# Moving the key copies, the key turnings and three exponentials inside a hand-written schedule of a hybrid decode step

## The chip, the cores and the metric

One core of one Trainium2 chip runs the whole step. The time is device microseconds of one launch. The kernel before takes 2246.21 us, the median of 3 runs (2242.72 to 2254.63).

## The reference: what is computed

One layer of a decoder with two head groups, for one new sequence of 512 tokens and for 8 decoding sequences with 4096 past tokens each. The part that matters here is, for each decoding sequence `b`, the attention over its paged cache (`cmp_attention`, `select_blocks` and `selected_attention` of the reference):

```
kc, vc = compress(cached keys), compress(cached values)   # windows of 32 rows, step 16
p_cmp  = softmax(q kc / 8);  o_cmp = p_cmp vc              # 255 compressed positions
imp    = group sums of p_cmp over blocks of 64 tokens
sel    = top_k(imp, 16)                                    # 3 blocks are forced
o_slc  = softmax(q k[sel] / 8) v[sel]                      # 16 chosen blocks, 961 positions
o_win  = softmax(q k_win / 8) v_win                        # the newest 512 rows
o      = g0 o_cmp + g1 o_slc + g2 o_win
```

The compression is the heavy part: `silu(rows . w1 + pe . w1) . w2` over all 4096 cached rows of each sequence. All numbers are float32. After the 8 sequences comes the output projection with a residual sum and a layer norm.

## The kernel before, in words

Three phases follow each other: the recurrent heads and the prompt (about the first 950 us), a middle phase to about 1150 us, and `decode_output_phase`, to which the change belongs.

**The places.** The decode part is one stream on TensorE of `NSTEP` = 128 steps, 16 for each sequence (8 for keys, then 8 for values). A step has three matmuls of 128x512 (`product(s, 0)` to `product(s, 2)`, L1592). Each of these 384 matmuls is a place; a sequence has 48 places. Behind the matmul of a place TensorE may do a unit of turning (`turn`, L1569: four transposes of cached rows into one of two PSUM banks `tb`), which ScalarE copies to SBUF in two instructions (L1835), after which VectorE takes differences (L1941, L1944). Four units make a group `Q`, and a group feeds two steps. Units stand in four of six places, so that they have to go through two banks: TensorE may not write a bank before the copy of the unit or piece before it is done.

**The pieces.** The attention of each sequence is cut into pieces, and a table gives each the place where all engines do their part of it. `AT` counts from the sequence's own first place, so 48 to 95 lie beside the compression of the next sequence and from 96 on beside that of the one after it; `LAST` is the same table for sequence 7. The function `program` walks over the places, and each of TensorE, ScalarE and VectorE runs it with its own functions: first its part of the matmul, then its part of the turning, then of the piece. Since an engine works strictly in order, a piece whose input is late holds all that stands behind it on that engine.

The pieces that the change touches:

- `fetch0` to `fetch3`: of the 16 chosen blocks a quarter at a time. ScalarE copies the keys of the gathered rows to `Kc` (L1894, L1895, L1897) and VectorE the values to `Vg` (L2082 to L2090). Both wait for the gather of that quarter. GpSimd issues the gathers (`chosen`, L1536), 5 indirect DMAs for the first quarter and 8 for each other, into two buffers in turn: quarter 2 may start when quarter 0 is copied, quarter 3 when quarter 1 is.
- `keys0` to `keys3`: TensorE turns `Kc` (L1698) into a bank, and VectorE copies the bank to `KgT` (`empty_keys`, L1807). There is one `Kc`, so `fetch1` waits for the turning of `keys0`, and so on.
- `scores`, `SCORES`, `WSCORES`: TensorE multiplies keys with queries (L1649), VectorE takes the maximum and its negative (L2006, L2097, L2103 and the lines behind), ScalarE the exponential with its sum (L1869, L1874, L1879).

Around them stand `bend` (L1850), the sigmoid of the compression on ScalarE at the places 23, 24, 47 and 48 of a sequence, whose output `sg` lies in the same memory as `Kc`; `finish` (L1964) on VectorE, which reads `sg`; `join_sum` (L1958); `keep_sum` (L1842). ScalarE has to load a table (ACT_TABLE_LOAD) when it goes from sigmoid to exponential or back.

**The other queues.** GpSimd also gathers the cached rows of the next sequence (`rows`, L1514, 32 indirect DMAs a sequence into `Xr` and `xT`), a quarter of a buffer at a time as its turning is done, and it issues them in between the gathers of `chosen` in one fixed order. SyncE loads the newest rows of the next sequence when the window piece `WVALUES` of a sequence is done (`window`, L1443 to L1449: 1 MB in, then 1 MB out).

```
if key[..] in TURNS: n = used.index(min(used)); put(pieces[t], n)     # bank of a piece
act.wait_ge(*landed(b, q)); ...; need(act, hs_r, bends[0])            # fetch on ScalarE
if keyed[0]: act.wait_ge(tr[bank], k + 1)                             # bend: Kc must be turned
```

Of the kernel before, what the change touches and what calls it, by code (L numbers as in the profile page):

```python
# [620 lines left out]
def need(eng, sem, n):  # L621

    if n > 0:
        eng.wait_ge(sem, n)
# [606 lines left out]
def decode_output_phase(nc, io, keep):  # L1231
# [14 lines left out]
    NJ, NSTEP = CD // 2, NB * CD  # L1246
# [5 lines left out]
    with ExitStack() as ctx:  # L1252
# [30 lines left out]
        acc, om = [sb(f"acc{n}", [R, KVH * DH]) for n in range(2)], sb("om", [P, KVH * DH])  # L1283
# [53 lines left out]
        AT = {  # L1337
            ("second", 0): 27, ("second", 1): 29, "queries": 25, "scores": 31, "weights": 34, "turned": 36,
            "sums": 37, "first": 38, "values": 39, "slots": 40, "bases": 41, "rows": 45,
            ("second", 2): 51, ("second", 3): 53, "fetch0": 55, "mix": 56, "acc": 57, "keys0": 59,  # L1340
            "fetch1": 62, "keys1": 64, "fetch2": 70, "keys2": 71, "fetch3": 80, "keys3": 81,
            "SCORES": 94, "SCALE": 96, "TURNED": 98, "VALUES": 100, "NEWEST0": 106, "NEWEST1": 108,
            "WSCORES": 109, "WSCALE": 113, "WTURNED": 115, "WVALUES": 116, "SUM": 117, "DONE": 122,
        }
# [7 lines left out]
        pieces = {}  # L1352
        for b in range(NB):
            for key, t in (AT | (LAST if b == NB - 1 else {})).items():
                t += 3 * CD * b
                t = t if t < 3 * NSTEP else 3 * NSTEP + 2 * (t - 3 * NSTEP)
# [14 lines left out]
        def landed(b, q):  # L1371

            return g_in[q % 2], 16 * (TAKEN[q % 2] * b + sum(GATHERS[q % 2:q + 1:2]))
# [10 lines left out]
        FETCH = "fetch0", "fetch1", "fetch2", "fetch3"  # L1384
# [4 lines left out]
        def unit(t):  # L1389

            s, n = divmod(t, 3)
            if s % 2 == 1 and n == 2:
                Q, u = (s + 3) // 2, 0
            elif s % 2 == 0:
                Q, u = s // 2 + 1, n + 1
            else:
                return None
            return (Q, u) if Q < NSTEP // 2 else None
# [4 lines left out]
        for t in range(3 * NSTEP + KT * TILES):  # L1403
# [4 lines left out]
            if t in pieces and pieces[t][0] in TURNS:  # L1408
                n = used.index(min(used))
                put(pieces[t], n)  # L1410
                used[n] = 2 * t + 3

        def program(eng, do):

            for s in range(NSTEP):
                for n in range(3):
                    do["product"](s, n)
                    then = unit(3 * s + n)
                    if then:
                        do["turn"](*then)  # L1420
                    name, which = pieces.get(3 * s + n, (None, None))
                    if name in do:
                        do[name](which)
            for u in range(KT * TILES):
                i, k = divmod(u, KT)
                do["output"](i, k)
                name, which = pieces.get(3 * NSTEP + u, (None, None))
                if name in do:
                    do[name](which)
                if k == KT - 1:  # L1430
                    do["end"](i)
# [390 lines left out]
        def _(act):  # L1822
# [59 lines left out]
            def fetch(q):  # L1882


                def do(b):
                    act.wait_ge(*landed(b, q))
                    if 4 * b + q:
                        bank, k = place[QUARTERS[q - 1], b if q else b - 1]
                        act.wait_ge(tr[bank], k + 1)
                    need(act, hs_r, bends[0])  # L1890
                    keyed[0] = QUARTERS[q], b
                    KVq = buffer(b, q)
                    if q == 0:
                        A(Kc[:, 0], forced(KVq, 0), ACT.Copy)  # L1894
                        A(Kc[:, 1], KVq[:, 1, :, 0:DH], ACT.Copy).then_inc(k_c, 1)  # L1895
                    else:
                        A(Kc[:], KVq[:, :, :, 0:DH], ACT.Copy).then_inc(k_c, 1)  # L1897

                return do
# [14 lines left out]
            for u in range(4):  # L1914
# [2 lines left out]
            program(act, {  # L1917
                "product": product, "turn": turn, "output": output, "end": lambda i: None,
                "scores": scores, "SCORES": chosen_scores, "WSCORES": newest_scores,
                **{FETCH[q]: fetch(q) for q in range(4)}})  # L1920
            gather(0)
            root(0, 0, P)
            root(1, 1, P)
# [414 lines left out]
```

## Time and profile before

| | us |
|---|---|
| median of 3 runs | 2246.21 |
| lowest, highest run | 2242.72, 2254.63 |
| the profiled execution | 2249.45 |
| its span, first to last instruction | 2247.6 |
| TensorE busy in the span | 2016.1 |
| VectorE busy | 915.7 |
| ScalarE busy | 707.9 |
| GpSimd busy | 629.6 |

The profiled execution took 1.85 us more than its span, and 3.2 us more than the median run. The rows further down are of this one execution. Times in them count from the start of its span. The decode part's 384 matmuls run from 1166.7 to 1979 us. A group of rows names the engine, the line, the operation, what is written and read, and how many; in brackets is the idle time of the engine before it and what ended it. "issue" means that nothing the profile shows was waited for, and "remote" that the semaphore's last writer could not be matched.

### The profile page before, as it was taken

The page shows a single profiled execution, that of the slowest core. Times are in us where ns is not written, and L with a number is a line of the kernel's source. Part 1 is how long each engine was busy: PE and PEld are TensorE (multiplying, and loading weights), DVE is VectorE, ACT ScalarE, POOL GpSimd, SP SyncE. Part 2 cuts the span into 40 slices and gives each one's busy share as a digit, 9 for nine tenths or more (in the row PEclk, how much of TensorE's full clock was granted, in tenths as well). Part 3 has the DMA queues.
Part 4 walks back from the last instruction along what each step waited for, and adds up shares of the span by engine and source line. Part 5 has one row for each costly group of instructions (what it writes and reads, how often), then busy time and mean ns, then how long its engine had stood idle before and what let it go on. Part 6 is the DMA issues. An engine that isn't in the chain of part 4 may idle for free. (4 is left out here: it accounts for less than half of the span.)

```text
span 2247.6 us, 24649 instructions
## 1 busy us (share of the span) xinstructions
PE 2016.1 (90%) x9303; PEld 1372.5 (61%) x9303; DVE 915.7 (41%) x1821; ACT 707.9 (31%) x1297; POOL 629.6 (28%) x649
## 2 busy tenths in 40 slices
PE   8999999999999999999968778677687878899997
PEld 7888888888888877777634334333343434434442
DVE  0445355454510144444434344445353545432126
ACT  0233112332200032332335444445354544510013
POOL 0000000000020034343545465555565555240000
PEclk9999999999999999999979889898888998999999
DMA  5232222222232211111155253545454453564114
GB/s 202 67 101 77 85 85 77 94 75 85 77 111 76 93 61 57 38 57 38 54 177 146 76 159 90 179 121 165 134 144 142 139 155 119 164 234 155 75 75 151
DMA packets 71076, 247.86 MB, mean 110 GB/s; under 512 B 11220, under 2 KB 28832, under 8 KB 56768
## 3 DMA queue, kind: packets, MB, share of 16 engines
q1 hardware_dynamic: 38344, 139.10, 17.8%
q0 software_dynamic: 31360, 103.32, 15.7%
q10 hardware_dynamic: 1280, 4.23, 0.5%
q8 instruction: 57, 0.93, 0.2%
q14 instruction: 35, 0.29, 0.0%
HBM read 224.64 MB, written 21.96 MB: 110 GB/s over the span
## 5 line engine op out<-in xcount | busy, mean ns | idle before, releaser
L292 PE MATMUL pj<-xT,strips 128*128 128x260 f32 x2368 | 532.6, 384 | 6.4 <-DMA xT<-d_xT 6.4
L292 PEld LDWEIGHTS pj<-xT,strips 128*128 128x128 f32 x2368 | 445.9, 191 | 72.3 <-issue 6.3
L1835 ACT ACTIVATE big<-dtb 64x512 f32<-64x512 f32 x512 | 302.8, 591 | 314.6 <-PE dtb L1569 172.2
L792 PE MATMUL pj<-xT,strips 128*128 128x260 f32 x1216 | 292.0, 388 | 0.0
L1592 PE MATMUL dpH<-big,w 128*128 128x512 f32 x512 | 287.3, 658 | 0.4 <-DVE hs L1958 0.4
L792 PEld LDWEIGHTS pj<-xT,strips 128*128 128x128 f32 x1216 | 222.4, 190 | 59.8 <-issue 30.1
L1018 POOL MEMSET kbd<- 128x128 f32 x1 | 0.2, 205 | 635.4 <-POOLq L126 635.4
L1569 PEld LDWEIGHTS dtb<-const,xT 128*128 128x128 f32 x512 | 65.3, 150 | 181.5 <-issue 87.5
L1941 DVE TENSOR_TENSOR big<-big 128x512 f32<-128x512 f32 x128 | 88.3, 689 | 212.5 <-ACT big L1835 174.2
L1569 PE MATMUL dtb<-const,xT 128*128 128x128 f32 x512 | 84.7, 292 | 99.9 <-DVE KgT L1807 79.2
L1044 POOL TENSOR_SCALAR old<-old,rd 128x128 f32<-128x128 f32 (+3 forms) x116 | 122.2, 1068 | 166.6 <-DVE rd L1153 166.6
L1536 POOL DMA_INDIRECT KV<-d_cache,gi x104 | 105.7, 1016 | 166.9 <-DVE gi L2072 89.9
L1514 POOL DMA_INDIRECT Xr<-d_cache,row x128 | 134.0, 1047 | 41.7 <-issue 38.7
L1569 PEld LDWEIGHTS dtb<-const,Xr 128*128 128x128 f32 x512 | 69.3, 155 | 122.4 <-issue 90.5
L1592 PE MATMUL dpH<-big 128*128 128x512 f32 x256 | 140.4, 631 | 0.0
L1514 POOL DMA_INDIRECT xT<-d_cache,row x112 | 109.3, 976 | 92.9 <-PE dtb L1569 64.3
L1536 POOL DMA_INDIRECT oT<-d_cache,gi x112 | 108.6, 969 | 85.1 <-DVE Vg L2085 53.1
L1592 PEld LDWEIGHTS dpH<-big,w 128*128 128x128 f32 x512 | 90.2, 206 | 62.7 <-issue 51.5
L1569 PE MATMUL dtb<-const,Xr 128*128 128x128 f32 x512 | 87.3, 299 | 36.4 <-ACT big L1835 20.9
L1611 PE MATMUL dpH<-xT,oT 128*128 128x512 f32 x256 | 113.6, 596 | 0.0
L1611 PE MATMUL dpH<-Xr,oT 128*128 128x512 f32 x256 | 113.0, 596 | 0.0
L988 ACT ACTIVATE PT<-mpT 128x512 f32<-128x512 f32 (+2 forms) x48 | 25.3, 526 | 206.3 <-PE mpT L880 196.5
(311 smaller groups left out, 2402.1 us busy)
## 6 DMA issues: line engine op xcount, KB each, us to landing
strips<-d_w_in SPq DMA_DIRECT2D x60, 1024.0 KB, 5.3
xT<-d_w_out SPq DMA_DIRECT2D x16, 1024.0 KB, 7.5
d_win_sample<-Wt SPq DMA_DIRECT2D x8, 1024.0 KB
Xr<-d_w_out SPq DMA_DIRECT2D x8, 1024.0 KB, 10.1
Wt<-d_win SPq DMA_DIRECT2D x8, 896.0 KB
xT<-d_xT SPq DMA_DIRECT2D x8, 520.0 KB, 8.9
Sold<-d_state SPq DMA_DIRECT2D x8, 512.0 KB, 5.5
vB<-v_rows ACTq DMA_DIRECT2D x8, 512.0 KB, 7.0
```

What stands on the lines that cost most here:

```text
L292: mm = nc.tensor.matmul(pj[b][:, a, 0:TH], w[b][:, k, :], xT[:, k, a * TH:(a + 1) * TH], start=(k == 0), stop=(k == KT - 1))
L792: mm = nc.tensor.matmul(bank(s)[:, n, 0:TH], w[s % 2][:, k, :], xT[:, k, n * TH:(n + 1) * TH], start=(k == 0), stop=(k == KT - 1))
L988: nc.scalar.activation(blocks(brs, 0, qt), pT[:, 0:len(brs) * (qt + 1) * P].rearrange("p (r c n) -> p r c n", r=len(brs), n=P), ACT.Copy). ...
L1018: nc.gpsimd.memset(kbd[:], 0.0).then_inc(zr, 1)
L1044: ins = nc.gpsimd.tensor_scalar(p, p, rd[U % 4][:, k:k + 1], None, ALU.mult)
L1514: pool.indirect_dma_start(out=X[par][:, r, :], out_offset=None, in_=pairs, in_offset=bass.IndirectOffsetOnAxis(ap=row[:, 2 * b + par, r:r ...
L1536: pool.indirect_dma_start(out=to, out_offset=None, in_=heads, in_offset=bass.IndirectOffsetOnAxis(ap=gi[b % 2][0:n, a:a + 1], axis=0),).th ...
L1569: mm = nc.tensor.transpose(tb[bank][:, i * P:(i + 1) * P], X[par][:, r, (2 * kind + hp) * P:(2 * kind + hp + 1) * P], ident)
L1592: mm = nc.tensor.matmul(pH[n][:], left, right, start=(j == 0), stop=(j == NJ - 1))
L1611: mm = nc.tensor.matmul(pH[i % 2][:], oT[:, k, t * P:(t + 1) * P], wo[c % 2][:, k, :], start=(k == 0), stop=(k == KT - 1))
L1835: ins = A(dst[:, :, :, hd], tb[bank][hd * DH:(hd + 1) * DH].rearrange("p (j h n) -> p j h n", j=2, h=2), ACT.Copy)
L1941: V.tensor_tensor(D1[:, s], D2[:, s], Or[:, s], ALU.subtract).then_inc(diff_r, 1)
```

## The change

Nothing is computed otherwise, and no instruction of data is added or removed. Three things move:

1. In `AT` (sequences 0 to 6) the copies `fetch0` to `fetch3` go from the places 55, 62, 70, 80 to 54, 59, 66, 72, and the turnings `keys0` to `keys3` from 59, 64, 71, 81 to 55, 62, 70, 76. `LAST` stays.
2. `program` takes a table `later`. For ScalarE alone the exponentials of `scores`, `SCORES` and `WSCORES` are done one place after the place where the other engines do their part (for sequence 7 as well).
3. A place can now hold two pieces of one engine; they are done in the order of the table.

```diff
         AT = {
             ("second", 0): 27, ("second", 1): 29, "queries": 25, "scores": 31, "weights": 34, "turned": 36,
             "sums": 37, "first": 38, "values": 39, "slots": 40, "bases": 41, "rows": 45,
-            ("second", 2): 51, ("second", 3): 53, "fetch0": 55, "mix": 56, "acc": 57, "keys0": 59,
-            "fetch1": 62, "keys1": 64, "fetch2": 70, "keys2": 71, "fetch3": 80, "keys3": 81,
+            ("second", 2): 51, ("second", 3): 53, "fetch0": 54, "keys0": 55, "mix": 56, "acc": 57,
+            "fetch1": 59, "keys1": 62, "fetch2": 66, "keys2": 70, "fetch3": 72, "keys3": 76,
             "SCORES": 94, "SCALE": 96, "TURNED": 98, "VALUES": 100, "NEWEST0": 106, "NEWEST1": 108,
             "WSCORES": 109, "WSCALE": 113, "WTURNED": 115, "WVALUES": 116, "SUM": 117, "DONE": 122,
         }
...
-        def program(eng, do):
-
+        def program(eng, do, later={}):
+
+            due = {}
+            for t, (name, which) in pieces.items():
+                if name in do:
+                    due.setdefault(t + later.get(name, 0), []).append((name, which))
             for s in range(NSTEP):
                 for n in range(3):
                     do["product"](s, n)
                     then = unit(3 * s + n)
                     if then:
                         do["turn"](*then)
-                    name, which = pieces.get(3 * s + n, (None, None))
-                    if name in do:
+                    for name, which in due.get(3 * s + n, ()):
                         do[name](which)
...
-                **{FETCH[q]: fetch(q) for q in range(4)}})
+                **{FETCH[q]: fetch(q) for q in range(4)}}, {"scores": 1, "SCORES": 1, "WSCORES": 1})
```

## Rows read from the trace of the kernel before

**Rows 1.** The page's first part: busy time, share of the span, instructions of each engine

```profile
PE 2016.1 (90%) x9303; PEld 1372.5 (61%) x9303; DVE 915.7 (41%) x1821; ACT 707.9 (31%) x1297; POOL 629.6 (28%) x649
```

**Rows 2.** Stretches of 48 places: length, busy us of each engine, clock, DMA share, GB/s

```profile
1567.00:1673.50 106.50, 81.50 (x344) 42.26 (x343) 48.11 (x106) 51.53 (x85) 59.87 (x61) 0.89 0.48 141
...
1882.00:1979.00 97.00, 80.09 (x323) 39.76 (x322) 45.93 (x102) 46.80 (x77) 32.14 (x33) 0.91 0.50 174
```

**Rows 3.** Waits of TensorE from 950 to 2100 us: total us, times, longest

```profile
PE dtb L1569 <- DVE KgT L1807: 79.2, 20, 12.6
...
PE dtb L1698 <- ACT Kc L1897: 22.6, 14, 2.6
```

**Rows 4.** Timeline round a `keys3`, places 31 to 35: start, us, engine, line

```profile
1538.80 1.28 ACT L1869 ACT_TABLE_LOAD   x1
...
1541.89 0.63 ACT L1897 ACTIVATE Kc<-oT 128x512 f32<-128x512 f32 x1
...
1542.58 0.99 PE L1698 MATMUL dtb<-const,Kc 128*128 128x128 f32 x4 [2.15 <-ACT Kc L1897]
...
1545.63 0.66 PE L1569 MATMUL dtb<-const,xT 128*128 128x128 f32 x4
```

**Rows 5.** Timeline round a `keys1`, places 16 and 17

```profile
1604.76 0.66 PE L1698 MATMUL dtb<-const,Kc 128*128 128x128 f32 x4 [1.08 <-ACT Kc L1897]
...
1607.82 0.66 PE L1569 MATMUL dtb<-const,xT 128*128 128x128 f32 x4 [1.54 <-DVE KgT L1807]
```

**Rows 6.** Timeline round a `keys2`, places 22 to 24: SyncE, TensorE, GpSimd, VectorE, ScalarE

```profile
1506.44 0.32 SPq L1443 DMA_DIRECT2D Wt<-d_win  x1
...
1508.75 0.60 PE L1698 MATMUL dtb<-const,Kc 128*128 128x128 f32 x4
...
1509.51 0.96 POOL L1514 DMA_INDIRECT xT<-d_cache,row  x1 [0.30 <-issue]
...
1522.06 0.69 DVE L1807 COPY KgT<-dtb 128x512 f32<-128x512 f32 x1 [9.79 <-remote]
1522.13 1.28 ACT L1850 ACT_TABLE_LOAD   x1 [14.22 <-remote]
...
1522.81 1.11 PE L1569 MATMUL dtb<-const,xT 128*128 128x128 f32 x4 [12.60 <-DVE KgT L1807]
```

**Rows 7.** TensorE's timeline at the same place of three other sequences

```profile
1416.52 1.12 PE L1569 MATMUL dtb<-const,xT 128*128 128x128 f32 x4 [12.02 <-DVE KgT L1807]
...
1838.26 1.11 PE L1569 MATMUL dtb<-const,xT 128*128 128x128 f32 x4 [10.43 <-issue]
...
1935.35 0.66 PE L1569 MATMUL dtb<-const,xT 128*128 128x128 f32 x4 [1.98 <-DVE KgT L1807]
```

**Rows 8.** Two stretches from a window load on, as in the view of rows 2

```profile
1506.40:1522.80 16.40, 3.81 (x15) 1.78 (x13) 5.77 (x10) 1.79 (x3) 9.79 (x11) 0.75 0.91 273
...
1929.60:1945.00 15.40, 11.49 (x45) 5.20 (x43) 10.89 (x24) 8.36 (x13) 2.15 (x3) 1.00 0.83 257
```

**Rows 9.** Timeline from `SCORES` on, place 46 to place 1 of the next sequence

```profile
1567.26 1.06 ACT L1874 ACTIVATE pg<-dpS,col 40x961 f32<-40x961 f32 x1 [4.51 <-DVE col L2098]
...
1568.43 1.28 ACT L1850 ACT_TABLE_LOAD   x1
1569.73 0.72 ACT L1850 ACTIVATE Kc<-hs,hb 128x512 f32<-128x512 f32 x1
...
1571.44 0.71 ACT L1850 ACTIVATE Kc<-hs,hb 128x512 f32<-128x512 f32 x1
...
1571.68 0.63 PE L1569 MATMUL dtb<-const,Xr 128*128 128x128 f32 x4 [2.17 <-issue]
```

**Rows 10.** The instructions of line L1850: table loads, ns min, median, max

```profile
L1850 ACT ACT_TABLE_LOAD  x15: 1283/1283/1283, 1195.1 to 1980.8; - x15
```

**Rows 11.** Timeline round `fetch0` at place 7 and the bank wait at place 11

```profile
1589.23 0.40 ACT L1894 ACTIVATE Kc<-KV 128x256 f32<-128x256 f32 x1
...
1595.06 0.63 PE L1569 MATMUL dtb<-const,xT 128*128 128x128 f32 x4 [1.48 <-DVE KgT L1807]
```

More of the change, by code:

```diff
@@ L1426, in program @@
                 do["output"](i, k)
-                name, which = pieces.get(3 * NSTEP + u, (None, None))
-                if name in do:
+                for name, which in due.get(3 * NSTEP + u, ()):
                     do[name](which)
```

## The prediction

> **What bounds the kernel now.** I read the busy times first: TensorE is busy for 90% of the span and every other engine for 41% or less [rows 1], so the end is set by TensorE's work and by the holes in it. Next the stretches of 48 places. A sequence takes 106.5 us with 81.5 us of TensorE's work in it, and the last one, which has the same matmuls but no rows of a next sequence to gather, 97.0 us with 80.1 [rows 2]. So some 25 us of each sequence are holes, and nine of them are absent when GpSimd has less to gather. ScalarE (51.5) and VectorE (48.1) are half idle [rows 2]: neither is a bound as a whole, only by its order. Last the list of TensorE's waits, which names two that belong to the moved pieces: 22.6 us in 14 waits for ScalarE's key copy, and 79.2 us in 20 waits for VectorE's copy of a bank to `KgT` [rows 3]. Most of the second is five long stalls, of 12.0, 12.6, 12.0, 10.2 and 10.4 us, at the one place behind `keys2` in the sequences that run from 1353 to 1882 us (the second of them in [rows 6], the first and the last in [rows 7]), 57.2 us together.
>
> **The waits for the key copy** (`fetch1`, `fetch3`). `fetch3` and `keys3` stand one place apart, so TensorE reaches the turning at once. ScalarE has the table load, the exponential of `scores` and two turning copies ahead of the key copy, and TensorE waits 2.15 us for it [rows 4]. At `keys1` it waits 1.08 us [rows 5]. Seven of each make the 22.6 us. With the change the gaps are 3 and 4 places in place of 2 and 1, and the exponential stands behind ScalarE's turning copy, not ahead of it. A place with its matmul and a turning takes over 1 us, so both waits go. What is late next is VectorE: behind `keys3` TensorE goes on into a turning without a long wait [rows 4], but behind `keys1` it waits another 1.54 us for `KgT` [rows 5], since VectorE's differences, which wait for ScalarE's turning copies, come before that copy. Those copies come forward by the exponential and its table load, about 2 us, so I expect this wait to stay and to end some 1 us earlier. I take the whole 22.6 us as gained. The bounds are nothing, if VectorE's copies take its place, and 22.6 plus seven times 1.54, 33 us.
>
> **`keys0` one place behind `fetch0`.** This makes a new wait of the kind of `keys1`, 1.08 us with two places between [rows 5]; with one place it is at most that and the turning copy that stands between, so I take the same 1.08 us a sequence as the price if nothing hides it, 8 us in all. But at place 11 TensorE stands 1.48 us for a bank that VectorE empties late [rows 11], and the transposes of `keys0` no longer stand there. That wait hides it, and I take nothing, with bounds of -3 and +8 us. GpSimd gains: it may start quarter 2 a place earlier, and quarter 3 directly behind it, because quarter 1 is copied at place 11, not 14. The gathers are then in SBUF well ahead of places 18 and 24, so neither `fetch2` nor `fetch3` waits for a landing. `fetch3` on ScalarE now stands behind the second sigmoid and must wait until VectorE has read `sg`; the turning copies between them cover that wait, and only its 0.63 us move into a busy stretch. That is in the bounds.
>
> **`keys2` one place earlier.** In the stall all three engines stand. TensorE's transposes of `keys2` are on record at 1508.75, but VectorE and ScalarE, which wait for them, go on only at 1522.06 and 1522.13, and TensorE at 1522.81 [rows 6]. The transposes take 0.60 us; whatever held their completion is not an engine's busy time. Beside the stall the window load is issued at 1506.44 and the gathers of the next rows begin at 1509.51 [rows 6]; the DMA engines are 91% busy at 273 GB/s in these 16.4 us [rows 8]. In the last sequence the same window load runs at the same place without row gathers behind it, the DMA share is 83%, TensorE is busy 11.5 of 15.4 us [rows 8], and the wait is 1.98 us [rows 7]. So I read the stall as held by the burst and not by the order of the pieces. With `keys2` at place 22 its turning finishes before the worst of it; TensorE then gets one more place done, a matmul and a turning of 1.02 and 0.60 us by their rows' kind, before the next turning is held in its turn: 1.6 us, five times, 8 us. The bounds are 0 and the full 57.2 us less one ordinary wait of 2 us in each, 47 us. In the other direction: row gathers are freed earlier by some 6 us through the earlier `fetch1`, and would overlap the window load from its start; the nearest row for what that can add is the whole difference between a stall and none, 10 us once.
>
> **The exponentials.** For `scores` and `WSCORES` the order against the sigmoids does not change, so neither does the number of table loads. For `SCORES` it does. Before, its exponential (place 46) comes ahead of both sigmoids (47, 48), one load for both [rows 9]; now it stands between them, after the sigmoid of place 47 and before that of 48. That is two more loads a sequence, in seven sequences (in the last, `SCORES` is elsewhere): L1850 would have 22 loads for 15 [rows 10] and L1874 seven for none. At 1.28 us each 14 loads are 18.0 us of ScalarE. Against it stands the 4.51 us for which ScalarE waits for the maximum at place 46 [rows 9]: the first sigmoid's table load and the sigmoid itself go into that wait. Laid out from the rows: the turning copies of place 47 stand between the two sigmoids and take 1.0 us (1569.73 + 0.72 to 1571.44); they could now start about when the exponential did, 1567.3, and end about 1568.4. Load, exponential (1.15 to the next load), load and second sigmoid (0.71) then end at about 1573.0; before, it ended at 1572.15 [rows 9]. So one turning copy comes 3 us earlier and the three after it 0.85 us later. TensorE waits 2.17 us at 1571.68 [rows 9] for the first of these and afterwards for the others, so the later ones count: +0.85 us, seven times, +6 us. The bounds are -15 us (the 2.17 us gained in all seven) and +18 us (all loads on the path).
> The Trainium skill (ScalarE: Activation LUTs, What ACT_TABLE_LOAD costs) gives about 1283 ns for the load and about 1380 ns more for a drain, 2.66 us a switch. By it the 14 loads would be an estimated 37 us, and it speaks against the change. The trace does not agree: the load starts at 1568.43 and the sigmoid at 1569.73 [rows 9], 1.30 us later with no drain between, so the sum goes by the row.
>
> **The sum.** -22.6 - 8 + 6 = -24.6 us. Against the profiled execution, 2249.45, that is 2224.8; it took 3.2 us more than the median of the runs, so the forecast against the median of 2246.2 is 2221.6, say **2222 us**.
>
> **The rivals.**
> *The stall dissolves.* If the five stalls come from the handing over at places 23 and 24 (`keys2`, its copy, the sigmoid and the next turning chained through one bank) and the burst is only beside it, moving `keys2` breaks the chain: another 39 us go, 2183 us, and 2173 if the VectorE wait behind `keys1` goes too. For it: all engines wait for this one turning. Against: the last sequence has the same chain and stalls 1.98 us [rows 7]. Chance 0.17.
> The Trainium skill (SBUF, State Buffer, section Who interferes with whom) says that DMA never contends with a compute engine; by that rule the burst could not hold TensorE, and this rival would be the likelier. Rows 7 and 8 speak against it.
> *Absorbed.* VectorE or the burst takes what ScalarE's copy gives: TensorE reaches the bank waits [rows 5, 11] and the stall, whose end hangs on transfers, earlier and waits there longer. 0 to 8 us are left, 2242 us. For it: 1.54 us of wait stand right behind one of the waits removed. Against: `keys3` has no such wait behind it [rows 4]. Chance 0.22.
> *Slower, through ScalarE at places 47 to 50.* The two loads (2.57 us) come whole onto the path, and TensorE, idle longer in this stretch, runs more of it at 1.2 GHz in place of 2.4: the granted clock is 0.89 of full over a sequence already [rows 2], and transposes and matmuls in such a stretch take twice as long (1.11 us against 0.66 for the same four transposes in [rows 7]). With some 7 us of work at the lower level that is 3.5 us more, 6 us a sequence, 42 in all. Less the 30.6 us that the other terms bring, +11, 2257 us. It decides from 4.4 us a sequence on. Against it: the first turning comes 3 us earlier. Chance 0.15.
> *The change does less than it says*, because a fetch waits for a landing or the planner gives a bad bank. Every piece still has its bank and its gather is over by my count; 0.04, either way of 2246.
>
> **How the numbers follow.** The forecast's own case (2205 to 2238) has 0.42. 0.5% is 11 us, and about what a measurement of this kernel can tell from no change. Faster by more than that, under 2235: 0.40 of the forecast, the 0.17, 0.06 of the absorbed case, 0.01 of the last: 0.64. Slower, over 2257: 0.08 of the slower rival, and with the tails of its bounds (+18 and a stall of 10 us more) and of the others 0.15. The rest is 0.21. The range reaches from 2180, which leaves out the lower half of the dissolved stall, to 2257, which leaves out the upper half of the slower rival: some 0.2 outside.
>
> **What would show it.** Right: no TensorE wait for L1897 but one of about 1 us at `keys0`; L1850 with 22 table loads and L1874 with 7; no idle time of 4.5 us before L1874; stalls of 9 to 12 us still there, one place later; a sequence of some 103 us. Wrong: stalls of 2 us (then the first rival), waits for L1807 grown by as much as those for L1897 fell (absorbed), or a granted clock under 0.89 and long waits for L1835 behind place 48 (slower).

## The result, and the profile after

| | before | after |
|---|---|---|
| median, us | 2247.27 (4 runs, 2242.72 to 2254.63) | 2284.61 (4 runs, 2281.16 to 2287.21) |
| span of the profiled execution | 2247.6 | 2282.8 |

The ratio is 1.0162, 95% interval [1.0131, 1.0193]: 37 us slower. I had forecast 2222 us, 25 us faster, and a range that ended at 2257.

The busy times of the changed kernel (first part of its page, as [rows 1]):

```profile
PE 2040.9 (89%) x9303; PEld 1381.6 (61%) x9303; DVE 913.9 (40%) x1821; ACT 727.4 (32%) x1311; POOL 619.8 (27%) x649
```

The work is the same but for ScalarE's 14 instructions more, the table loads; its busy time is 19.5 us longer. The decode part's 384 matmuls now take 844.5 us from first to last start, where they took 811.5. The first of them starts at 1171.1 us for 1166.7, so 4.4 us of the longer span arise ahead of the part that was changed. TensorE's waits from 950 to 2150 us (as [rows 3]; the code of the decode part stands two lines further down, so L1807 is L1809, L1698 is L1700, and the copies of `fetch1` to `fetch3` are at L1899, `fetch0`'s at L1897):

```profile
PE dtb L1571 <- DVE KgT L1809: 81.7, 23, 10.7
PE dtb L1571 <- issue: 37.9, 19, 3.9
PE dpK L1687 <- DVE rhs L2064: 24.5, 7, 3.7
PE dtb L1571 <- ACT big L1837: 19.6, 9, 3.5
...
PE dtb L1700 <- ACT Kc L1897: 9.4, 7, 5.0
```

All 14 waits for the key copies of `fetch1` and `fetch3` are gone: no wait for L1899 is left. The seven that stand here, for L1897, are new and belong to `keys0` at place 7. The 80 us behind VectorE's copy are not gone, and the long stalls in them are not where they were. Timeline round the new place 17, in the sequence that starts at 1573.4 us (the last line is the same place in the last sequence):

```profile
1606.35 0.94 POOL L1538 DMA_INDIRECT oT<-d_cache,gi  x1 [0.30 <-issue]
...
1609.38 0.60 PE L1571 MATMUL dtb<-const,Xr 128*128 128x128 f32 x4
...
1610.97 0.63 PE L1700 MATMUL dtb<-const,Kc 128*128 128x128 f32 x4 [0.98 <-issue]
...
1613.87 0.68 DVE L2105 TENSOR_REDUCE col<-dpS 40x1 f32<-40x512 f32 x1 [7.11 <-remote]
...
1614.96 0.90 POOL L1538 DMA_INDIRECT oT<-d_cache,gi  x1 [0.30 <-issue]
1618.82 1.19 ACT L1837 ACTIVATE big<-dtb 64x512 f32<-64x512 f32 x2 [8.00 <-remote]
...
1623.44 1.11 PE L1571 MATMUL dtb<-const,xT 128*128 128x128 f32 x4 [9.27 <-DVE KgT L1809]
...
1627.29 0.95 POOL L1516 DMA_INDIRECT xT<-d_cache,row  x1 [11.42 <-PE dtb L1571]
...
1630.91 0.32 SPq L1445 DMA_DIRECT2D Wt<-d_win  x1
...
1961.71 1.12 PE L1571 MATMUL dtb<-const,xT 128*128 128x128 f32 x4 [10.61 <-DVE KgT L1809]
```

TensorE's transposes of 1609.38 should have been over at 1609.98, but ScalarE, which waits for them, goes on only at 1618.82; the reduction on VectorE is held in the same way. I call this a hold: TensorE's instructions are on record, their semaphore reaches the other engines up to 9 us late, and the stall of [rows 6] is one too. The trace also has the times of the semaphore updates themselves, and they say the same: the updates of TensorE's work that ended at 1608.49, 1609.98 and 1614.17 are at 1613.84, 1618.80 and 1618.93. In the same stretch ScalarE's copy that ended at 1610.82 let TensorE go on at 1610.97. So TensorE's updates are late against the ends on record, and ScalarE's is not. The ends of matmuls are modelled in a profile, so these rows can't tell whether the work itself or only its update was late. The window load (1630.91) and the row gathers (1627.29), in which I had seen the cause, come after it here. The hold ends behind the last of the quarter's gathers (1614.96 + 0.90), within 3 us of it.

**Where the 37 us arose.** The median over the sequences 2 to 6 of each place's duration, summed by stretch: places 0 to 16 took 36.4 us before and 39.7 after, places 17 to 36 took 50.0 and 46.3, places 37 to 47 took 18.9 and 26.2. So the moved stall is no worse than the old one was (11.2 us at place 17 for 13.9 at place 24), and place 33, where `keys3` stood, is 3.2 us shorter. The loss is 3.3 us in the first stretch, nearly all of it at the places 47 and 0 to 4, where the later exponential of `SCORES` falls, and 7.3 in the last, where there was no hold before. That is 6.9 us a sequence; of the other sequences, 1 is 9.6 us shorter than before and the last 7.7 us longer. Windows of the three stretches in the sequence that starts at 1573.4, after (columns as in [rows 2]):

```profile
1573.40:1613.10 39.70, 31.90 (x144) 16.67 (x143) 12.70 (x25) 18.68 (x30) 23.22 (x25) 0.91 0.33 98
1613.10:1659.50 46.40, 33.35 (x135) 17.19 (x133) 21.85 (x50) 25.41 (x41) 24.34 (x26) 0.85 0.57 170
1659.50:1686.10 26.60, 19.67 (x66) 8.35 (x66) 13.49 (x32) 10.34 (x17) 13.29 (x14) 0.87 0.46 131
```

The timeline in the last one:

```profile
1661.34 0.66 PE L1571 MATMUL dtb<-const,Xr 128*128 128x128 f32 x4 [0.70 <-issue]
...
1665.36 0.95 POOL L1516 DMA_INDIRECT xT<-d_cache,row  x1 [0.30 <-issue]
1667.32 1.20 ACT L1837 ACTIVATE big<-dtb 64x512 f32<-64x512 f32 x2 [7.16 <-remote]
...
1668.74 0.21 DVE L2033 COPY sc<-dpK 4x62 f32<-4x62 f32 x1 [7.52 <-remote]
...
1678.31 1.05 PE L1687 MATMUL dpK<-rhs,const 4*128 4x32 f32 x4 [3.72 <-DVE rhs L2064]
```

Again a hold that ends behind the last gather of a row without a pause (here 12 row gathers from 1651.6 on). It delays VectorE's choice of the blocks (`sc` to `rhs`), and TensorE waits for that as well: 24.5 us over the sequences, where it was 13.9.

### The profile page after: what moved, and what is told of

It reads as the page before. It is cut to its first block and busy times, and to the rows that moved or that the text cites. A ratio compares the mean times of both kernels' runs of the same rounds, so it can differ in the third digit from the quotient of the medians.

```text
span 2282.8 us, 24663 instructions
## 1 busy us (share of the span) xinstructions
PE 2040.9 (89%) x9303; PEld 1381.6 (61%) x9303; DVE 913.9 (40%) x1821; ACT 727.4 (32%) x1311; POOL 619.8 (27%) x649
## 5 line engine op out<-in xcount | busy, mean ns | idle before, releaser
L1538 POOL DMA_INDIRECT KV<-d_cache,gi x104 | 101.1, 972 | 206.9 <-DVE gi L2074 108.8
L1594 PE MATMUL dpH<-big 128*128 128x512 f32 x256 | 152.6, 681 | 0.0
L1571 PE MATMUL dtb<-const,Xr 128*128 128x128 f32 x512 | 82.5, 286 | 52.9 <-issue 18.4
```

Of the source, the lines that this page charges most:

```text
L1538: pool.indirect_dma_start(out=to, out_offset=None, in_=heads, in_offset=bass.IndirectOffsetOnAxis(ap=gi[b % 2][0:n, a:a + 1], axis=0),).th ...
L1571: mm = nc.tensor.transpose(tb[bank][:, i * P:(i + 1) * P], X[par][:, r, (2 * kind + hp) * P:(2 * kind + hp + 1) * P], ident)
L1594: mm = nc.tensor.matmul(pH[n][:], left, right, start=(j == 0), stop=(j == NJ - 1))
```

## The experiments

In five jobs, each on one chip, beside the kernel before. Expectations stand as they were written before each run.

**One: the two halves of the change, and the exponentials one by one.** The edits against the changed kernel, in short form:

```diff
 places_only:   {"scores": 1, "SCORES": 1, "WSCORES": 1}  ->  {}
 later_only:    AT as before
 later_scores:  AT as before, {"scores": 1}
 later_SCORES:  AT as before, {"SCORES": 1}
```

> The new places of the copies and turnings, with ScalarE's exponentials where they were. Theory A (the exponentials are the loss: the one of the compressed scores stands behind a turning copy, so the chain to the chosen rows comes later, and the one of the chosen scores brings two table loads): the loss of 37 us goes, and the waits for the key copy stay away, so 2220 to 2245 us. Theory B (the long stall of TensorE moves to where keys1 stands and brings more with it, the exponentials are small): 2265 to 2285 us, with long stalls at place 17.

> The old places, with all three exponentials one place later on ScalarE. Theory A: most of the loss is here, 2270 to 2290 us, places 37 to 46 longer by about 7 us a sequence, the stall still at place 24. Theory B: 2240 to 2260 us.

> The old places; only the exponential of the compressed scores one place later. No table load is added. Theory A: if the chain to the chosen rows is what counts, at least half of the loss of later_only is here: 2255 to 2275 us, TensorE's wait for rhs at place 45 longer by 2 us a sequence. If the table loads count, within 5 us of before.

> The old places; only the exponential of the chosen scores one place later: 14 more table loads, 18 us of ScalarE. If the table loads are on the path: 2256 to 2265 us and places 0 to 5 longer. If they are covered by the idle time that they replace: within 5 us of before, or below it.

Measured, against a median of 2253.17: places_only 2282.64, ratio 1.0113 [1.0053, 1.0172]; later_only 2257.55, 1.0029 [1.0002, 1.0057]; later_scores 2245.36, 0.9960 [0.9934, 0.9986]; later_SCORES 2256.51, 1.0023 [0.9998, 1.0047]. The new places alone lose 25 us (12 to 39), the three later exponentials alone 6.5 (0 to 13). `SCORES` one place later measured +5 us, with an interval from 0 to 11 that just includes nothing; `scores` one place later gains 9, from 3 to 15. The third, `WSCORES`, was not run by itself. By difference (6.5 + 9 - 5) it, or what it does together with the others, would cost some 11 us, and my sum had it at nothing.

**Two: are the gathers or the window load the cause?** before_norows and after_norows leave out the gathers of the rows of sequences 1 to 7 in the kernel before and the changed one, so that all sequences compress sequence 0's rows; before_nowin leaves out the window's load and write-back for sequences 1 to 7; fetch3_78 has `fetch3` at 78 for 80 and nothing else.

> The kernel before, with the gathers of chosen rows left out for sequences 1 to 7 (TensorE attends to sequence 0's rows each time, so the output is another). It tells whether the stalls of 10 to 14 us a sequence need these gathers. Theory 'gathers hold TensorE's semaphore updates': the one long wait of a sequence (13.9 us at place 24 in the median of sequences 2 to 6) falls under 4 us, and the matmul part gets 40 to 70 us shorter: 2180 to 2210 us. Rival 'the stall is made by the order of the pieces alone': it stays over 9 us, and the time is 2235 us or more, since nothing else that TensorE does is taken away. My prediction's cause (the burst of window load and row gathers together) would leave the window load alone: stall under 6 us.

> The changed kernel with the same gathers left out. Gather theory: the wait of 11.2 us at place 17 falls under 4 us, and the loss of 36 us against the kernel before goes: within 10 us of the run of the kernel before without gathers. Rival 'order of the pieces': the stall at place 17 stays over 9 us and the time stays 25 us or more above that run.

> The kernel before, without the load of the window rows and the write-back of the window for sequences 1 to 7. By my prediction's reading (the DMA burst, the window load in it, holds the key pieces after keys2) the wait of 13.9 us at place 24 shrinks to 6 us or less and the time falls by 35 to 60 us, to about 2200. By what the changed kernel showed (its stall of 11.2 us stands ahead of the window load's issue) the window load is not the cause: the stall stays over 9 us and the time within 15 us of 2250.

> The kernel before with fetch3 alone moved from place 80 to 78, so that the key copies of the fourth quarter find their rows present. It prices the term of 15 us that my sum gave to the ScalarE wait of 2.15 us there, by itself. If that wait lies on the path: 2247 - 15 = 2232 us. If it is absorbed by TensorE's other waits or by a hold that comes in any case: 2242 to 2252 us. If the earlier gather meets a hold of its own: above 2255 us.

Measured: 2139.60, ratio 0.9985 [0.9967, 1.0003]; 2131.59, 0.9946 [0.9926, 0.9967]; 2141.43, 0.9995 [0.9972, 1.0017]; 2137.11, 0.9974 [0.9956, 0.9992]. But in this job the unaltered kernel before took 2144.29 us (31 runs, 2136.55 to 2156.21), 109 less than in the first, and there leaving out gathers or window changes next to nothing. In no profile of this job is there a hold, fetch3_78's with all its gathers and window loads included. So whether holds occur hangs on something outside the kernel, which stays the same through a job; the runs here show two kinds of job, with holds (before near 2245) and without (near 2144). My first two questions stayed open here, and the third job asked one again.

fetch3_78 shows one thing well, by TensorE's waits in before_nowin (its `fetch3` as in the kernel before; first fence) and in fetch3_78 (second):

```profile
PE dtb L1571 <- DVE KgT L1809: 33.9, 23, 2.0
PE dtb L1700 <- ACT Kc L1899: 21.6, 14, 2.1
...
PE dtb L1571 <- ACT big L1837: 14.8, 10, 2.2
```

```profile
PE dtb L1569 <- DVE KgT L1807: 51.7, 27, 2.6
...
PE dtb L1698 <- ACT Kc L1897: 6.7, 7, 1.1
```

14.9 us of waits for ScalarE's copy went, all at place 33, and 17.8 us of waits for VectorE's came, at place 35. In the median sequence place 33 is 2.4 us shorter and place 35 is 2.4 us longer. The time fell by 6 us (2 to 9), not by 15.

**Three: the other kind of job, again.** after_again is the changed kernel itself, places_again is places_only, norows_again is before_norows; places_scores is the changed kernel with `{"scores": 1}` alone.

> The changed kernel itself, beside the kernel before, on one more chip. The runs of the second job met another chip: there the kernel before takes 2144 us, not 2247, its long wait at place 24 is 3.4 us instead of 13.9, and the parts left out (row gathers, window load) change its time by less than 0.2%. Theory 'the holds belong to the chip': on a chip where the kernel before takes about 2145 us, the changed kernel has no wait over 8 us at place 17 and takes 2125 to 2145 us (ratio 0.99 to 1.00); on a chip where the kernel before takes about 2250, it takes 2275 to 2295 (ratio 1.01 to 1.02). Rival 'the loss is the schedule's on any chip': ratio 1.013 or more on either chip.

> The new places of gathers and key copies, and of the three exponentials only that of scores one place later. From the places' durations of the runs without gathers: the new places save some 6 us a sequence from place 12 on, the two later exponentials SCORES and WSCORES cost some 6 us at places 2 to 11. Chip without holds: 2095 to 2115 us against 2145, the fastest version. Chip with holds: the stall at place 17 decides, 2265 to 2285 us. Rival 'the early places lose their time to something else than the two exponentials': no faster than the changed kernel, within 5 us of it, on either chip.

> The kernel before without the gathers of chosen rows, as in the run before_norows, on whichever chip this job meets. On a chip with holds: theory 'the holds need the row gathers' gives 2145 to 2180 us with no wait over 5 us at place 24; rival 'they come from the schedule or other transfers' gives 2240 to 2255 with the wait at place 24 still over 9 us. On a chip without holds it says nothing new: 2137 to 2143.

> The new places alone, all exponentials where they were. On a chip without holds: the terms of my sum for the key copies (22.6 us) and more, since no long stall comes in their way: 2095 to 2120 us against 2145. On a chip with holds: about 1.011 times the kernel before, as in the first job. Rival 'the new places lose by themselves on any chip': ratio above 1.005 on both.

This job had holds: before 2238.98. Measured: after_again 2267.28, ratio 1.0133 [1.0101, 1.0164]; places_scores 2261.61, 1.0118 [1.0088, 1.0147]; places_again 2253.24, 1.0068 [1.0044, 1.0091]; norows_again 2172.38, 0.9710 [0.9676, 0.9744], with 3.4 us at place 24. In the kernel before the long stall needs the row gathers.

This job also prices the parts of the change beside each other. Of the 28 us that after_again loses, the new places are 14; `scores` one place later adds 8, and `SCORES` and `WSCORES` together 6. So here the exponentials are half of the loss, and the intervals of places_again and after_again don't touch. With the old places `scores` later had paid. Its 8 us have a place in the trace: in the stretch 37 to 47 places_scores takes 25.4 us and places_again 21.5.

**Four: what carries the hold to place 17?** q01_only has the new places of quarters 0 and 1 alone, q1_kept those of 0, 2 and 3; both without `later`. after_norows2 is after_norows.

```diff
 q01_only:  fetch0 54, keys0 55, fetch1 59, keys1 62 | fetch2 70, keys2 71, fetch3 80, keys3 81
 q1_kept:   fetch0 54, keys0 55, fetch1 62, keys1 64 | fetch2 66, keys2 70, fetch3 72, keys3 76
```

> Of the change only the first two quarters' places: fetch0 54, keys0 55, fetch1 59, keys1 62; quarters 2 and 3 and the exponentials as before. Theory 'the hold follows the gather of the last quarter of chosen rows, which the copy fetch1 sets free': on a chip with holds the wait of 10 to 12 us is at place 17 and that at place 24 is gone (under 4 us); time above the kernel before's, ratio 1.005 to 1.02. Rival 'the hold follows the key pieces of the third quarter (keys2)': the long wait stays at place 24. On a chip without holds (kernel before near 2145): no wait over 5 us anywhere, time within 10 us of the kernel before.

> Of the change the places of quarters 0, 2 and 3 (fetch0 54, keys0 55, fetch2 66, keys2 70, fetch3 72, keys3 76), with fetch1 62 and keys1 64 as before; exponentials as before. Gather theory: on a chip with holds the long wait stands 5 to 12 us behind the start of the last quarter's gather, so between places 21 and 26 and not at 17; some 20 us of the 25 that keys3 at its earlier place saves are kept, ratio 0.99 to 1.00. Rival 'any shift of the key pieces moves the hold to the first of them': wait over 8 us at place 17 or earlier, ratio above 1.005. On a chip without holds: 2115 to 2135 us.

> The changed kernel without the gathers of the next sequence's chosen rows (output then of sequence 0's rows). In the changed kernel these gathers start some 2 us behind the end of the long wait at place 17, so if they are needed for it, it is by what they did a sequence earlier. On a chip with holds: theory 'holds need the row gathers' gives no wait over 5 us at place 17 and 2140 to 2185 us, as for the kernel before without them (2172 there). Rival 'the hold at place 17 comes from the four quarters' own gathers': it stays over 8 us, 2210 us or more. On a chip without holds: 2130 to 2134, as measured.

A job with holds (before 2248.78). q01_only: 2264.97, ratio 1.0064 [1.0042, 1.0086], 11.2 us at place 17 and 4.3 at place 24. q1_kept: 2282.15, 1.0127 [1.0090, 1.0163], 3.1 us at place 17 and 7.4 at place 23 in the median, 12.1 in the sequence that starts at 1583.1. So the hold goes with `fetch1`, whose copy sets free the gather of quarter 3; but my time for q1_kept was wrong. after_norows2: 2217.42, 0.9852 [0.9812, 0.9892], still 11.2 us at place 17: in the changed kernel the row gathers are not needed for it, and of the two readings that I wrote down, the rival's is the right one. Its timeline, and windows round the end of the hold:

```profile
1570.67 0.63 PE L1696 MATMUL dtb<-const,Kc 128*128 128x128 f32 x4 [0.51 <-issue]
...
1576.09 0.91 POOL L1538 DMA_INDIRECT oT<-d_cache,gi  x1 [0.30 <-issue]
1579.89 1.19 ACT L1833 ACTIVATE big<-dtb 64x512 f32<-64x512 f32 x2 [9.37 <-remote]
```

```profile
1572.00:1578.50 6.50, 1.87 (x5) 0.57 (x3) 0.83 (x2) 0.00 (x0) 3.78 (x5) 0.93 0.34 92
1579.00:1585.00 6.00, 0.49 (x3) 0.49 (x4) 3.75 (x8) 3.24 (x5) 0.00 (x0) 0.50 0.00 0
```

The hold ends as the last gathers drain (DMA share 0.00 from 1579.0 on); during it the DMA engines are a third busy, at 92 GB/s.

**What the holds have in common.** For each of TensorE's semaphore updates that a trace can match with its instruction (sequences 2 to 7) I take how long it came behind the instruction's end, and how many gathers GpSimd had issued without a pause of 1 us at that time. In the 13 kept traces of jobs with holds:

| gathers issued in the row so far | updates | over 1 us late |
|---|---|---|
| none | 1910 | 38 |
| 1 to 4 | 1279 | 15 |
| 5 to 8 | 965 | 335 |
| 9 or more | 571 | 508 |

The largest delay is 13.6 us. All 215 updates that were over 5 us late fall in rows of 12 or more, and they arrived at most 3.2 us behind the row's last gather. ScalarE's and VectorE's updates in the same traces (7766) were never over 0.02 us late. In the seven kept traces of jobs without holds TensorE's 3066 updates were at most 0.06 us late, in rows of up to 61 gathers.

Three kernels left traces in both kinds of job, and before_nowin can stand for the fourth, so each stretch's holds can be read off as a difference, with the reservation that the two traces come from different jobs (medians over sequences 2 to 6, us; "row" is the longest row of gathers in the stretch with less than 1 us between two, from GpSimd's timeline of sequence 4 in the job with holds):

| kernel | 0 to 16 | row | 17 to 36 | row | 37 to 47 | row |
|---|---|---|---|---|---|---|
| before, holds / before_nowin, none | 36.4 / 35.2 | 13 | 50.0 / 38.0 | 16 | 18.9 / 19.1 | 8 |
| after, holds / after_third, none | 39.7 / 37.6 | 13 | 46.3 / 35.4 | 16 | 26.2 / 19.2 | 12 |
| after_norows2 / after_norows | 39.9 / 39.0 | 13 | 45.2 / 35.4 | 16 | 17.4 / 17.4 | 0 |
| norows_again / before_norows | 36.4 / 35.2 | 13 | 40.1 / 37.9 | 8 | 19.1 / 19.1 | 8 |

Rows of 8 cost 0 to 2 us, the rows of 16 in the middle stretch 10 to 12, the 12 in the last 7, the 13 across a sequence's border 1 to 2. The other runs with holds agree in sign in the last stretch: q01_only (rows of 8) 18.8 us, q1_kept (12) 22.3, places_again (12) 21.5, places_only (12) 22.6, places_scores (12) 25.4, after_again (16) 25.6. So a row of 12 costs some 2 to 4 us there, and 6 to 7 where `scores` comes one place later; what a hold costs depends also on which instructions it meets. In the kernel before, the 16 are quarter 3's eight and the first eight row gathers (40.2 to 60.0 us in its sequence, with 6.4 us of pause ahead); in the changed kernel they are quarters 2 and 3 (22.6 to 42.5), because `fetch1` no longer comes later than the end of quarter 2. And in the last stretch, where eight and eight were 2.4 us apart, there are now 12 in a row. That comes with the early `keys3`: q1_kept has it and the 12, q01_only has neither. I read it as TensorE's saved wait closing the pause, which was argued and not tried by itself. Nor was the window load left out in a job with holds; the hold at place 17 ends before it starts.

**Five: pauses put in.** pause_rows is the kernel before with a pause ahead of the row gathers; places_paused is places_only with that and one ahead of quarter 3. after_third is the changed kernel. The edits, shortened, with comments added:

```diff
+if b > 2 and (q, par) == (0, 1):            # rows: wait for the transposes of DONE, place 26
+    bank, k = place["DONE", b - 3]; pool.wait_ge(tr[bank], k + 1)
+if q == 3:                                  # chosen, places_paused alone: wait for those of keys1
+    bank, k = place[QUARTERS[1], b]; pool.wait_ge(tr[bank], k + 1)
```

> The kernel before, with one wait more on GpSimd: from sequence 3 on, the gathers of the next sequence's chosen rows start only when the transposes of the old DONE piece (place 26) have run, so that some 5 us lie between the eight gathers of the last quarter and the 32 of the rows. Theory 'a hold comes when more than about 12 gathers follow one another without a pause': on a chip with holds the wait of 13.9 us at place 24 falls under 5 us; the rows end some 5 us later and the next selection's first gather with them, which costs at most 5 us a sequence; sum 2185 to 2225 us, the first version faster than the kernel before by more than 1%. Rival 'the hold comes when row gathers run beside the key pieces, pause or none': it comes 5 us later, at places 25 to 27, and the time is 2245 us or more. On a chip without holds: 2145 to 2180 us, slower.

> The new places of copies and key pieces (exponentials as before), with that pause and a second one: the last quarter's gather waits for the transposes of keys1, so that some 5 us lie between the eight gathers of quarter 2 and the eight of quarter 3. Gather theory on a chip with holds: no wait over 5 us at place 17 nor at 24, and since the early keys3 saves 3 us a sequence, 10 to 20 us under pause_rows. Rival 'the hold belongs to the key pieces': the wait at place 17 stays over 8 us and the time over 2250. On a chip without holds: 2110 to 2160 us.

> The changed kernel once more, to see it on a chip without holds, if this job meets one (kernel before near 2145 us): then 2125 to 2145 us, no wait over 8 us at place 17, ratio 0.99 to 1.00; if the schedule itself loses, 1.01 or more. On a chip with holds (kernel before near 2245): ratio 1.01 to 1.02 as measured twice.

This job had no holds (before 2144.90), so the pauses had nothing to prevent. pause_rows: 2141.06, 0.9985 [0.9966, 1.0005]; places_paused: 2134.58, 0.9953 [0.9937, 0.9968], with one execution of 7149.63 us among its eight, for which nothing was found. pause_rows costs nothing even here, where I had expected a slower kernel; whether pauses help in a job with holds wasn't tried. after_third: **2131.89, 0.9946 [0.9927, 0.9965]**: by the ratio, here the change makes the kernel 12 us faster. Its waits as above, and its wait at place 17:

```profile
PE dtb L1571 <- DVE KgT L1809: 35.1, 21, 2.7
PE dtb L1571 <- ACT big L1837: 23.0, 10, 3.6
...
PE dtb L1700 <- ACT Kc L1897: 5.1, 7, 0.7
```

```profile
1531.12 0.60 PE L1700 MATMUL dtb<-const,Kc 128*128 128x128 f32 x4
...
1535.94 0.66 PE L1571 MATMUL dtb<-const,xT 128*128 128x128 f32 x4 [1.64 <-DVE KgT L1809]
```

and the windows of the three stretches of its sequence 4, with 48 gathers in a row in them and no hold:

```profile
1495.70:1533.30 37.60, 31.71 (x145) 16.79 (x144) 14.34 (x30) 20.64 (x33) 21.72 (x22) 0.91 0.32 98
1533.30:1568.70 35.40, 29.95 (x135) 15.42 (x133) 20.29 (x47) 23.42 (x39) 27.50 (x26) 1.00 0.73 225
1568.70:1587.90 19.20, 17.41 (x65) 7.86 (x65) 13.26 (x31) 10.39 (x17) 13.06 (x13) 0.91 0.62 176
```

More DMA work at a time (225 GB/s for 170) and gathers closer together, and TensorE is held by neither.

## Why the prediction was wrong

**The step that failed** is "I read the stall as held by the burst and not by the order of the pieces". The stall at `keys2` is a hold, and in the kernel before it needs the row gathers (norows_again); so much was right. Wrong was that it belongs to the place at which the window load and the row gathers start. It goes where a long row of gathers runs, and which gathers follow one another is set by the places that the change moves. My witness was the last sequence, with the window load and without row gathers. What set it apart was that quarter 3's eight gathers had no row gathers right behind them, not a lighter burst: in the changed kernel the same sequence, again without row gathers, stalls for 10.6 us. I took -8 us over all. The stretch 17 to 36 gave -3.7 us a sequence, of which 3.2 are place 33's and so the key copy's, and the stretch 37 to 47, which my sum did not have at all, +7.3. Some 3 to 4 of these 7.3 come with the later exponential of `scores`, which my sum put at nothing (places_scores against places_again, 25.4 for 21.5).

**The key-copy waits, -22.6 us.** The waits went as forecast: none of the 14 is left in places_only, after or after_third. Whether their time comes back depends on where VectorE's copy of the bank stands. In fetch3_78, with `keys3` left at its old place, it takes the wait's place, 17.8 us for 14.9. "`keys3` has no such wait behind it [rows 4]" was a wrong argument for that case: there was none because ScalarE's wait covered it. With the whole change and no holds this does not happen. From before_nowin to after_third the waits for VectorE's copy go from 33.9 to 35.1 us only, and place 33 stays 3.2 us shorter. With holds, the early `keys3` also goes with the row of 12 gathers in the last stretch; beside the old exponentials that row costs about what place 33 gains (places_again: 21.5 us for 18.9).

**`keys0`, 0 us.** TensorE waits for its copy seven times in after_third, 5.1 us in all, 0.7 each; its wait behind VectorE at place 11 falls from 9.0 to 5.7. That is within my bounds.

**The exponentials, +6 us.** ScalarE has 22 table loads at L1852 and seven at L1876, as laid out. later_SCORES measured +5 us, [0, 11]. That this is near my 6 is in part luck: I had 0.85 us a sequence for the turning copies behind place 48, and the places 47 and 0 to 4 are 3.0 us longer in its trace (3.1 in after_third against before_nowin), of which later places give some back. Load to exponential is 1.30 us here too:

```profile
1574.83 1.28 ACT L1876 ACT_TABLE_LOAD   x1
...
1576.13 1.06 ACT L1876 ACTIVATE pg<-dpS,col 40x961 f32<-40x961 f32 x1
...
1577.30 1.28 ACT L1852 ACT_TABLE_LOAD   x1
1578.59 0.72 ACT L1852 ACTIVATE Kc<-hs,hb 128x512 f32<-128x512 f32 x1
```

The 1380 ns of drain that the Trainium skill adds (ScalarE: Activation LUTs, What ACT_TABLE_LOAD costs) do not appear here: where nothing else is waited for, the load starts 0.02 us behind the instruction before it and the activation 1.29 to 1.30 us behind the load's start, in the other sequences too. So the row was the right price for a load. What I left out is `scores` and `WSCORES`, for which I counted table loads and nothing else. `scores` one place later measured -9 us with the old places, and +8 beside the new ones in another job, where the two intervals just touch. `WSCORES` was not run alone.

**The rivals.** The stall did not dissolve. "Absorbed" named what fetch3_78 showed, but not what the whole change did. The slower rival had its sign right, and part of its place: places 47 and 0 to 4 cost some 3 us a sequence against its 6, but the larger part is the new hold at the places 37 to 47. The rule of the Trainium skill (SBUF, State Buffer, Who interferes with whom), that DMA never contends with a compute engine, is not refuted as it stands: in jobs without holds nothing is held at 225 GB/s, and in a hold it is TensorE's semaphore update that comes late, by up to 13.6 us. My weighing of rule against trace was too coarse: the trace showed coincidence with a burst, not its cause.

**Two readings of the rows were off**, neither in the sum. Between the sequence and the last one the holes differ by 8 us (25.0 and 16.9), not nine. The transposes of 1.11 us against 0.66 took 1.7 times as long, not twice.

**In a job without holds** the change gives -12 us [-16, -8], of the -24.6 of my sum. The key copies' waits fell by 16.5 us with next to nothing in their place. What grew is the wait for ScalarE's turning copies behind the sigmoids, from 14.8 to 23.0 us, nearly all of it at place 2 of a sequence (place 1 before), where the exponential of `SCORES` now stands ahead of them. By these waits the term that was mis-sized there is that of the exponentials. It was not run by itself in such a job: places_paused has the old exponentials and was no faster than after_third, but its pauses make the places 17 to 19 2.4 us longer.

**Still open:** what decides whether a job has holds (the fourth and fifth ran on a chip of the same number and differ; whether it was the same chip isn't known), why a long row of gathers delays TensorE's semaphore updates there and not those of ScalarE and VectorE, whether TensorE's work itself ends late with them, and whether pauses cure it. No version was shown to beat both kernels in jobs of either kind; later_scores is ahead of the kernel before by 0.4% in one with holds.

## What to carry to other kernels

A stall in which all engines stand and the instruction waited for is long on record belongs to no piece: before costing its move, list what else runs through it in several sequences, GpSimd's gathers with their pauses too, and ask how the change will regroup them. A wait removed from the bounding engine can also remove a pause from the queues it releases. Where a trace has the times of semaphore updates, compare them with the ends of the instructions, engine by engine: that shows whose updates are late and beside what. Price every part of a change beside the other parts too: `scores` later gained 9 us with the old places and cost 8 with the new. And time a change of under 2% in more than one job: this one is 1.6% slower in one and 0.5% faster in another.

## What the runs showed of the hardware

- The same kernel takes 2239 to 2253 us in three jobs (and 2247 in the runs of the result) and 2144 to 2145 in two, each time in all its executions. In the sequences 2 to 6, 12 of some 13 us a sequence are in the places 17 to 36, where 16 gathers run in a row (50.0 for 38.0 us).
- TensorE's semaphore updates can come 5 to 13.6 us behind the end on record of their instruction while indirect DMAs are issued every 1.25 us, 12 or more in a row, with the DMA engines a third busy (0.34 of their time, 92 GB/s, in after_norows2); they come at most 3.2 us behind the last gather. During the first four gathers of a row 15 of 1279 updates are over 1 us late, from the ninth on 508 of 571. ScalarE's and VectorE's updates stay within 0.02 us.
- In other jobs 48 gathers in a row, at 225 GB/s, hold nothing: TensorE's updates stay within 0.06 us.
- A hold costs clock as well: in the stretch with the hold the granted clock is 0.85, in the same stretch without it 1.00.
